# A layered decoder step on one core: the squares of a norm's blocks added on VectorE, and their mean taken by TensorE behind 24 matmuls of the next layer

## What is computed

```
x += ConformerConv(rms_norm(x))                       layer 0
x += SwiGLU(rms_norm(x))                              layer 0, d_ff = 2816
k, v = split(rms_norm(x) @ w_kv)                      shared keys and values
x += SlidingWindowAttention(rms_norm(x) @ w_q, k, v)  layer 1
x += Top2of8_MoE(rms_norm(x))                         layer 1, d_ff = 3584 for each expert

def rms_norm(x, g):
    y = xf * lax.rsqrt(jnp.mean(xf * xf, axis=-1, keepdims=True) + EPS)
    return (y * g.astype(jnp.float32)).astype(x.dtype)
```

## Time and profile before

| | |
|---|---|
| median of 3 runs | 1552.03 us (1550.81 to 1553.04) |
| the profiled execution | 1551.22 us, its span 1549.4 us |
| PE busy | 1518.6 us, 98% |
| DVE, ACT, POOL busy | 1219.6 (79%), 967.8 (62%), 115.5 us (7%) |
| mean granted clock of PE | 0.985 of full speed |
| mean matmuls `bank<-sq,con` L404 | 64 records, 20.3 us busy |
| router squares `bank<-con,sq` L667 | 48 records, 6.0 us busy |

### The profile page before, as it was taken

One profiled execution on the slowest core, in us unless ns is written; L12 is line 12 of the kernel. 1 busy time (PEld: TensorE's weight loads), 2 busy tenths in 40 slices (PEclk: granted clock), 3 DMA queues, 4 the chain that ended last, 5 costly groups with the idle time before them and its releaser, 6 DMA issues.

```text
span 1549.4 us, 22063 instructions
## 1 busy us (share of the span) xinstructions
PE 1518.6 (98%) x7901; PEld 1287.0 (83%) x7901; DVE 1219.6 (79%) x1241; ACT 967.8 (62%) x1068; POOL 115.5 (7%) x99
## 2 busy tenths in 40 slices
PE   8998999999989989999999999999999999999998
PEld 6997999999975978888888888888888888888777
DVE  6996545546696468898889888889889889888886
ACT  6654443344564356777677677777677677767764
POOL 2001011011320010000000000000000000000000
PEclk9999999999998989999999999999999999999999
DMA  9940344444540559989979999998998998998992
GB/s 350 164 141 28 109 163 177 152 154 148 187 140 34 194 223 364 369 314 407 392 304 407 395 352 352 397 385 318 404 379 318 421 368 311 423 375 304 412 373 112
DMA packets 66547, 438.48 MB, mean 283 GB/s; under 512 B 8101, under 2 KB 10405, under 8 KB 15936
## 3 DMA queue, kind: packets, MB, share of 16 engines
q1 hardware_dynamic: 57600, 412.38, 68.0%
q0 software_dynamic: 5552, 19.36, 5.1%
q10 hardware_dynamic: 3344, 6.05, 1.1%
HBM read 423.73 MB, written 15.03 MB: 283 GB/s over the span
## 4 chain that ended last, share of the span: by engine, by line
PE 93%; DVE 3%; DMA 2%; ACT 1%; POOL 1%; issue 0%; DVEq 0%; ACTq 0%; SPq 0%; POOLq 0%
PE bank L379 28%; PE bank L381 27%; PE bank L380 27%; PE bank L430 3%; PE bank L790 2%; DMA land<-in_w_expert 1%; PE bank L404 1%; PE bank L642 0%; PE bank L722 0%; PE bank L728 0%; PE bank L631 0%; PE bank L671 0%; PE bank L594 0%; PE bank L616 0%; DMA bias<-rel_rows 0%
## 5 line engine op out<-in xcount | busy, mean ns | idle before, releaser
L1497 DVE TENSOR_TENSOR w_lo<-land,w_hi 128x2048 fp32r<-128x2048 f32 x224 | 504.2, 2289 | 77.2 <-ACT w_hi L1095 75.5
L1095 ACT CAST w_hi<-land 128x2048 fp32r<-128x2048 f32 x224 | 418.4, 1914 | 5.8 <-issue 3.4
L379 PE MATMUL bank<-w_hi,xe_hi 128*128 128x512 f32 x896 | 364.5, 407 | 1.6 <-DVE xe_lo L1583 1.0
L381 PE MATMUL bank<-w_hi,xe_lo 128*128 128x512 f32 x896 | 354.4, 396 | 0.0
L380 PE MATMUL bank<-w_lo,xe_hi 128*128 128x512 f32 x896 | 353.0, 394 | 0.0
L1596 DVE TENSOR_TENSOR d_lo<-land,d_hi 128x2048 fp32r<-128x2048 f32 x112 | 256.7, 2292 | 44.5 <-ACT d_hi L1098 43.7
L1098 ACT CAST d_hi<-land 128x2048 fp32r<-128x2048 f32 x112 | 213.9, 1911 | 123.2 <-PE bank L381 119.8
L381 PEld LDWEIGHTS bank<-w_hi,xe_lo 128*128 128x128 f32 x896 | 168.4, 188 | 39.2
L379 PEld LDWEIGHTS bank<-w_hi,xe_hi 128*128 128x128 f32 x896 | 169.1, 189 | 36.1 <-DVE xe_lo L1583 1.2
L380 PEld LDWEIGHTS bank<-w_lo,xe_hi 128*128 128x128 f32 x896 | 169.0, 189 | 34.1
L379 PE MATMUL bank<-d_hi,heT_hi 128*128 128x512 f32 x448 | 177.5, 396 | 1.1 <-DVE heT_lo L1628 1.1
(11 more groups left out here) (266 smaller groups left out, 2094.3 us busy)
## 6 DMA issues: line engine op xcount, KB each, us to landing
land<-in_w_expert SPq DMA_DIRECT2D x336, 1024.0 KB, 6.5
land<-in_w_dense SPq DMA_DIRECT2D x54, 1024.0 KB, 4.8
rel_rows<-rb POOLq DMA_DIRECT2D x1, 3072.0 KB, 36.0
bias<-rel_rows ACTq DMA_DIRECT2D x4, 512.0 KB, 5.8
y_rows<-zero_rows POOLq DMA_DIRECT2D x3, 512.0 KB, 10.6
X<-in_x SPq DMA_DIRECT2D x4, 288.0 KB, 5.9
out_y<-X SPq DMA_DIRECT2D x4, 288.0 KB, 2.2
Us<-in_state POOLq DMA_DIRECT2D x1, 1088.0 KB, 9.6
```

The lines of the kernel that those rows point to most:

```text
L379: pe.matmul(out, w[0], x[0], start=start, stop=False)
L381: return pe.matmul(out, w[1], x[0], start=False, stop=stop)
L1095: act.copy(w_hi[n % RING][:], land[(DENSE + u) % LAND][:]).then_inc(hi_done, 1)
L1497: dve.tensor_tensor(w_lo[n % RING][:], land[slot][:], w_hi[n % RING][:].bitcast(F32), ALU.subtract).then_inc(split, 1)
```

## The change

For norms 2, 3 and 4, ACT squares block 0 into a new buffer `sq_sum`, and blocks 1 to 7 into `sq` as before. DVE adds the squares of blocks 1 to 6 to `sq_sum` (`add_square`, six instructions a norm, 18 in all), so `sq_sum` holds seven blocks. PE takes the mean with two matmuls instead of eight: one over `sq_sum`, one over the square of block 7. In norms 2 and 3 these two stand behind the first 24 matmuls of the next layer (`mean_of_sum`), in norm 4 in the last block's router sums (`squares_of`). Norms 0 and 1 stay. The first four outputs of the dense layer get a wait of their own for the X that frees their bank (before, the means' waits covered it). ACT's squares wait for DVE's adds instead of PE's means.

```diff
@@ -130,6 +130,7 @@
+        sq_sum = sb("sq_sum", [P, T])
@@ -217,6 +218,7 @@
+        sq_added = sem("sq_added")
@@ -301,6 +303,10 @@
 
         USED_BEFORE = KT_D + 2 * (FH + DOWN_UNITS - 1)
 
+        def added(q, k):
+
+            return (KT_D - 2) * (q - 2) + k
+
         def h_number(a, k):
 
 
@@ -403,6 +409,13 @@
                     pe.wait_ge(sq_ready, KT_D * (q - 1) + k + 1)
                 pe.matmul(STAT[:, 0:T], c("mean_d"), sq[:, k % 2, :], start=(k == 0),
                           stop=(k == KT_D - 1)).then_inc(sq_summed, 1)
+
+            def mean_of_sum(q):
+
+                pe.wait_ge(sq_added, added(q, KT_D - 2))
+                pe.matmul(STAT[:, 0:T], c("mean_d"), sq_sum[:], start=True, stop=False)
+                pe.wait_ge(sq_ready, KT_D * q)
+                pe.matmul(STAT[:, 0:T], c("mean_d"), sq[:, 1, :], start=False, stop=True).then_inc(sq_summed, 1)
 
             def keep_busy(out, n):
 
@@ -472,10 +485,6 @@
                         wait_h(1, k)
                     last = mm3(bank[d % 4][:, 0:T], wblock(n, KT_D * (d % 2) + k), H(k), k == 0, k == KT_D - 1)
                 last.then_inc(pw2_done, 1)
-                if d >= 2:
-                    mean_part(2, d - 2)
-            mean_part(2, KT_D - 2)
-            mean_part(2, KT_D - 1)
 
             for half in range(2):
                 for i in range(FH):
@@ -486,10 +495,14 @@
                         pe.wait_ge(a_raw, f - 1)
                     for part in range(2):
                         out = bank[2 * (f % 2) + part][:, 0:T]
+                        if f < 2:
+                            pe.wait_ge(x_conv, KT_D // 2 + 2 * f + part + 1)
                         for k in range(KT_D):
                             if f == 0 and part == 0:
                                 wait_h(2, k)
                             last = mm3(out, wblock(n, KT_D * part + k), G(k), k == 0, k == KT_D - 1)
+                        if f == 0 and part == 0:
+                            mean_of_sum(2)
                     last.then_inc(used, 1)
                 for d in range(KT_D):
                     if KT_D * half + d >= 2:
@@ -506,10 +519,6 @@
                         if blk == BPU - 1 and i < FH - 1:
                             last.then_inc(used, 1)
                     last.then_inc(down_done, 1)
-                    if half == 1 and d >= 2:
-                        mean_part(3, d - 2)
-            mean_part(3, KT_D - 2)
-            mean_part(3, KT_D - 1)
 
             pe.wait_ge(split, U_K + 1)
             for t in range(2):
@@ -518,6 +527,8 @@
                         wait_h(3, k)
                     last = mm3(bank[t][:, 0:T], wblock(U_K, KT_D * t + k), H(k), k == 0, k == KT_D - 1)
                 last.then_inc(kq_done, 1)
+                if t == 0:
+                    mean_of_sum(3)
 
             def head_mean(i):
 
@@ -655,18 +666,23 @@
                 turn_probs(s)
             attend(len(STEPS) - 1)
 
+            def squares_of(src):
+
+                for i, (t0, nt) in enumerate(TT):
+                    pe.matmul(STAT[0:nt, i:i + 1], src[:, t0:t0 + nt], c("mean_d")[:, 0:1], start=False, stop=False)
+
             def route_sums(k):
 
-                pe.wait_ge(sq_ready, KT_D * 3 + k + 1)
                 pe.wait_ge(hm_ready, k + 1)
                 if k == 0:
 
                     pe.wait_ge(pick_zero, 1)
                     pe.matmul(STAT[:, 0:32], ident, pick[:, 0, 0:32], start=True, stop=False)
-                for i, (t0, nt) in enumerate(TT):
-                    last = pe.matmul(STAT[0:nt, i:i + 1], sq[:, k % 2, t0:t0 + nt], c("mean_d")[:, 0:1],
-                                     start=False, stop=False)
-                last.then_inc(sq_summed, 1)
+                if k == KT_D - 1:
+                    pe.wait_ge(sq_added, added(4, KT_D - 2))
+                    squares_of(sq_sum)
+                    pe.wait_ge(sq_ready, KT_D * 4)
+                    squares_of(sq[:, 1, :])
                 for i, (t0, nt) in enumerate(TT):
                     last = pe.matmul(STAT[0:nt, 8 + NE * i:8 + NE * i + NE], Hm[:, k, t0:t0 + nt], router[:, k, :],
                                      start=False, stop=False)
@@ -859,13 +875,16 @@
 
             def square(q, src, k):
 
-                if KT_D * q + k >= 2:
+                if q == 1:
                     act.wait_ge(sq_summed, KT_D * q + k - 1)
-                act.activation(sq[:, k % 2, :], src[:, k, :], ACT.Square).then_inc(sq_ready, 1)
+                elif k >= 3:
+                    act.wait_ge(sq_added, added(q, k - 2))
+                dst = sq_sum[:] if q >= 2 and k == 0 else sq[:, k % 2, :]
+                act.activation(dst, src[:, k, :], ACT.Square).then_inc(sq_ready, 1)
 
             def root(q):
 
-                act.wait_ge(sq_summed, KT_D * (q + 1))
+                act.wait_ge(sq_summed, KT_D * (q + 1) if q < 2 else 2 * KT_D + q - 1)
                 act.activation(sd[:], STAT[:, 0:T], ACT.Sqrt, bias=c("eps")).then_inc(sd_ready, 1)
 
             def h_hi(a, k, dst):
@@ -1225,6 +1244,13 @@
                 dve.wait_ge(h_hi_ready, m + 1)
                 dve.tensor_tensor(lo[:, k, :], raw[:, m % RAW, :], hi[:, k, :].bitcast(F32),
                                   ALU.subtract).then_inc(h_ready[1], 1)
+
+            def add_square(q, k):
+
+                dve.wait_ge(sq_ready, KT_D * (q - 1) + k + 1)
+                if k >= 2:
+                    dve.wait_ge(sq_added, added(q, k - 1))
+                dve.tensor_tensor(sq_sum[:], sq_sum[:], sq[:, k % 2, :], ALU.add).then_inc(sq_added, 1)
 
             def gained(a, gain, k):
 
@@ -1342,6 +1368,8 @@
                     h_lo_odd(2, d - 2, G_hi, G_lo)
                 if d % 2 and d < KT_D - 1:
                     lo_to(U_PW2 + RING + d // 2 + 1)
+                if 1 <= d <= KT_D - 2:
+                    add_square(2, d)
             h_lo_odd(2, KT_D - 1, G_hi, G_lo)
             inverse_root(2)
             lo_to(U_GU[0] + RING)
@@ -1378,6 +1406,8 @@
                         gained(4, "g_attn", d)
                         if d >= 1:
                             h_lo_odd(4, d - 1, G_hi, G_lo)
+                        if 1 <= d <= KT_D - 2:
+                            add_square(3, d)
                 if half == 0:
                     lo_to(U_GU[1] + 3)
             h_lo_odd(4, KT_D - 1, G_hi, G_lo)
@@ -1514,6 +1544,8 @@
                 dve.tensor_scalar(Hm[:, d, :], X[:, d, :], v("g_moe", d), None, ALU.mult).then_inc(hm_ready, 1)
                 if d % 2 and d < KT_D - 1:
                     expert_lo(0, *FIRST_UNITS[d // 2])
+                if 1 <= d <= KT_D - 2:
+                    add_square(4, d)
 
             LG, SEL, EX, DIFF, TMP, COMB = (lg[:, i] for i in range(6))
             dve.wait_ge(sd_ready, 5)
```

## The result

| | before | after |
|---|---|---|
| median | 1552.26 us (1550.81 to 1553.04, 6 runs) | 1539.22 us (1538.17 to 1540.63, 6 runs) |
| span of the profiled execution | 1549.4 us | 1536.5 us |
| PE busy | 1518.6 us | 1502.2 us |

The account below looks back on a forecast made before the run. The last-ending chain was taken as 93% TensorE (PE). Gains of 0.8, 0.6 and 3.5 at norms 2, 3 and 4 made 4.9 us, less 1.4 and 1.0 for the clock: 2.5 less, median 1549.5 us, range 1546.6 to 1552.8.

Parts of the forecast that it names:

- A fall of the clock elsewhere would make the total wrong with the steps right: Closing sign: PE's clock falling anywhere but behind the waits at norms 2 and 3 would spoil only the total.
- Norm 2, PE idle 2.4 us, released by G_lo: Dense layer's first 24 matmuls: PE ready at 176.4 waits 2.4 us for DVE's G_lo of block 5 at 178.8.
- The adds stand in front of X and delay it: Norm 2, DVE: adds between subtraction and X put X of block 7 at 177.5, half a microsecond later.
- Gain 0.8 before the clock: Norm 2: the dense layer's second 24 matmuls begin at 181.0 instead of 181.8, gaining 0.8 us.
- The fall takes 1.4: Norm 2: behind the idle stretch PE runs at 1.2 GHz instead of 2.4, a loss of 1.4 us.
- Norm 3, idle 2.5, fall of the clock, -0.4: K's first 24 matmuls: PE waits 2.5 us for POOL's H_lo; gain 0.6, less 1.0 for the clock.
- I take X 7 and the 396.4 as they are: Norm 3: X of block 7 unmoved, POOL's H_lo of block 7 done at 396.4, despite DVE beginning some blocks earlier.
- Norm 4, 3.5: Router's norm: 8 sets of squares' matmuls become 2, 0.58 us each, 3.5 us gained, all showing in the chain.
- A mean costs 0.48: Second projection of the convolution (pw2): one mean matmul behind each block takes 0.48 us of PE.
- Adds at 0.46, few of them beside POOL: DVE's adds take 0.46 us each, as few meet a POOL operation; the other end was 0.83.
- the prediction's first rival: The clock holds at one place (3.5 to 3.9 us gained, 1548.3) or both (4.9, 1547.1); chance 0.35.
- DVE doesn't keep pace: Denies the rival that adds fit idle time and G_lo, H_lo are ready: 8.5 us gained, 1543.5; chance 0.06.

Follow-up runs that it names:

- e2_noshift: The changed kernel with sq_sum above every other buffer, so that all of them lie where they lay before the change; 1548.58 us, ratio 0.9985.
- e15_back: The changed kernel with 128 unused bytes behind sq_sum, so that xe_hi - w_hi is again 128 modulo 256; 1546.72 us, ratio 0.9976.
- e18_warm: The changed kernel with four extra matmuls into an unused bank ahead of PE's wait for block 5 of G at norm 2; 1538.08 us, ratio 0.9919.
- e4_norms23: The changed kernel with norm 4 as before, so only norms 2 and 3 changed; buffers as in the changed kernel; 1543.57 us, ratio 0.9946.
- e3_norm4: The changed kernel with norms 2 and 3 as before, so only the router's norm changed; buffers as in the changed kernel; 1539.16 us, ratio 0.9924.
- e1_pad: The kernel before with one unused buffer of 1152 bytes between sq and stats, no instruction different; 1543.1 us, ratio 0.9942.
- e20_last: Norms 2, 3, 4 changed, norm 2's add behind the next block's gained form, sq_sum above all phases, unused buffers behind sq, ahead of xe_hi and heT_hi; 1533.08 us.
- e19_order: The changed kernel with the add of block d-1 behind the gained form of block d in norms 2 and 3, not ahead of X; 1540.45 us, ratio 0.9929.

## Why the prediction was wrong

**The total: a term that was never in the sum.** The change was costed instruction by instruction, "what it removes, adds and moves", and of the 12 to 13 us some 9 came from none of these. The first line of the diff, a buffer ahead of most others, moved the experts' tokens by 1152 bytes against their weights and 2688 matmuls became 3 to 4 ns shorter. The step that failed is the list of what the change does. Neither the sum, nor a rival, nor the range held a change of pace in code that the diff doesn't touch. "A fall of the clock elsewhere would make the total wrong with the steps right" named the kind of error, and not this one.

**The edit itself: 2.5 forecast, 2.3 and 3.7 measured** with the old distance modulo 256 (e2_noshift, e15_back). That agreement is partly luck, as the steps show: norms 3 and 4 gave some 2 us more than forecast, and 1.5 us were lost again behind PE's last product, a term that the sum didn't have.

- *Norm 2, PE idle 2.4 us, released by G_lo:* right, 2.13. *The adds stand in front of X and delay it:* right, X of block 7 at +21.85 (22.0 forecast); taking them from there brought it to +20.6. *Gain 0.8 before the clock:* right; with the clock held (e2_noshift) the stretch is 0.83 shorter than before. *The fall takes 1.4:* right in size, 1.5 (e18_warm). Net 0.84 lost against 0.6 forecast, in one pair of traces; e4_norms23 and e15_back have 105.01 and 104.14, and six kernels with the old norm 2 and the old distance 103.20 to 104.62, by the length of the half clock in pw2.
- *Norm 3, idle 2.5, fall of the clock, -0.4:* wrong in the size of the wait. The profile shows 1.40 idle (counted from where the next matmul would have started, as the prediction did, 1.6), and the clock held. K's square was the last wait as forecast (0.65 at the head's mean; 0.5 forecast). Gain 0.84 (1.1 to 1.2 in e2_noshift, e4_norms23 and e15_back) instead of a loss of 0.4. "I take X 7 and the 396.4 as they are" was the step: H_lo was done at 395.26, 146.65 behind the first down matmul where 147.38 were taken, since DVE began some blocks earlier (X of block 7 stands 144.32 behind that matmul instead of 145.17), as the prediction itself had said before it set this aside.
- *Norm 4, 3.5:* mis-sized; 4.37 in the trace and 3.9 between the medians of e3_norm4 and e1_pad. Per block 0.58 for the squares and 0.10 more in the router's own group behind them, which no row with the squares in place could show; and at the end two matmuls at half clock (0.2).
- *A mean costs 0.48:* right; from pw2's first matmul to the dense layer's first are 28.81 instead of 32.61, and 8 x 0.48 = 3.84.
- *Adds at 0.46, few of them beside POOL:* right in size, 0.45 to 0.46 for all 18, and wrong in the reason. At norm 3 all six ran beside a subtraction of POOL, and POOL's took the loss (1.14 instead of 0.81). G_lo of block 7 beside POOL's H_lo still takes 0.82. So the sentence of the Trainium skill (SBUF — State Buffer, section "SBUF: two separate sides") agrees again, and decided nothing: of the subtractions of POOL that grew PE waited for one, and for 0.13 us (that of block 6).

**The clock.** The prediction took a fall at both places and gave 0.35 to its holding. The same idle time of 2.13 to 2.15 us was followed by a full fall in the changed kernel and e15_back (nine steps in 2.33 and 2.32 us), and by none in e2_noshift (1.29 us); e4_norms23, with 2.13, lies between (1.78). The waits of 1.40, 1.41, 1.59 (e20_last) and, at norm 3 in e19_order, 1.72 were followed by none. So the rule of the Trainium skill (TensorE: Matmul & The Clock Gate, section "Why this matters for your kernels"), that only longer gaps need be avoided, held in one execution and not in others, at gaps of 2.13 to 2.15 us; a fixed charge for a gap was too simple, as the prediction's first rival said.

**The other rivals.** DVE doesn't keep pace (PE waits at both places); the clock doesn't stay down; the router's gain arrives in full.

## What to carry to other kernels

And work taken off a dense PE only pays where the next layer can start earlier: six means less (2.9 us of PE's work) bought about one microsecond at norm 3, and at norm 2 a loss or a gain of 0.8 with the clock, since the chain through DVE (and, at norm 3, POOL) sets that start, while the same idea in the router, with nothing to start early, paid in full.
